# A two-layer hybrid diffusion step: one ScalarE copy per layer-norm tile in place of two activations, and private weight buffers for one up-projection unit

## The reference

```python
def post_norm(x, y, g, b):
    return layer_norm(ALPHA * x + y, g, b)

def modulate(x, shift, scale):
    return x * (1 + scale) + shift

def conv_ffn(h, w_up, conv_w, conv_b, w_down):
    u = dwconv3(h @ w_up, conv_w, conv_b)
    g, val = jnp.split(u, 2, axis=-1)
    return (jax.nn.silu(g) * val) @ w_down

# in each layer i, for context (p) and latent (s) tokens
xs = post_norm(xs, mod_s[2] * ys, ln_g[i, 0], ln_b[i, 0])
hs = modulate(xs, mod_s[3], mod_s[4])
fs = conv_ffn(hs, ffn_w_up[i], ffn_conv_w[i], ffn_conv_b[i], ffn_w_down[i])
xs = post_norm(xs, mod_s[5] * fs, ln_g[i, 1], ln_b[i, 1])
```

## Time and profile before

| | us |
|---|---|
| median of 3 timed runs | 1999.53 (1999.06 to 1999.94) |
| the profiled execution, its own time | 1995.32 |
| the span of its trace | 1993.4 |
| TensorE matmul busy | 1831.9 (92% of the span) |
| TensorE weight load busy | 1682.0 (84%) |
| VectorE busy | 1148.0 (58%) |
| ScalarE busy | 804.4 (40%) |
| GpSimd busy | 645.8 (32%) |
| TensorE waiting for GpSimd's L467, layer 0 and layer 1 | 3.3 and 3.4, once each |

### The profile page before, as it was taken

How to read it: one execution, slowest core, us unless ns; L and a number is a source line. 1 busy time by engine, 2 the same in 40 slices (tenths; PEclk the granted TensorE clock), 3 DMA queues, 4 the chain that set the end, 5 groups by cost and what they waited for, 6 DMA issues and landing times.

```text
span 1993.4 us, 31127 instructions
## 1 busy us (share of the span) xinstructions
PE 1831.9 (92%) x11636; PEld 1682.0 (84%) x11636; DVE 1148.0 (58%) x1634; ACT 804.4 (40%) x1203; POOL 645.8 (32%) x278
## 2 busy tenths in 40 slices
PE   6999999996889999999997799999789999999995
PEld 2338888885779999999996789888779999999995
DVE  6994667665447772277724645354456773177723
ACT  5982554554253331133325445355343332133323
POOL 0002212122355443333344231223355433333341
PEclk9999999997889999999998899999989999999998
DMA  9992111110112222122221111121111222122221
GB/s 386 359 362 72 49 40 48 51 44 18 42 43 74 71 74 87 53 74 74 90 73 32 48 56 46 48 64 38 32 53 62 75 75 80 57 74 74 86 73 53
DMA packets 49054, 164.94 MB, mean 83 GB/s; under 512 B 5584, under 2 KB 11216, under 8 KB 48848
## 3 DMA queue, kind: packets, MB, share of 16 engines
q1 hardware_dynamic: 42640, 159.68, 24.0%
q10 hardware_dynamic: 6336, 4.20, 0.7%
HBM read 159.12 MB, written 4.74 MB: 82 GB/s over the span
## 4 chain that ended last, share of the span: by engine, by line
PE 79%; DVE 9%; ACT 5%; issue 2%; DVEq 2%; DMA 2%; POOL 1%; ACTq 0%; SPq 0%; POOLq 0%
PE pj L511 66%; DVE alo L1537 2%; PE mO L881 2%; DMA awr<-in_w_ada 2%; PE psS L634 2%; PE psO L676 2%; PE psT L650 1%; DVE X L1620 1%; ACT h32t L1028 1%; PE prow L550 1%; PE psT L659 1%; DVE pr L1718 1%; DVEq L1619 1%; PE mS L837 1%; PE mT L844 1%
## 5 line engine op out<-in xcount | busy, mean ns | idle before, releaser
L408 POOL TENSOR_TENSOR wlo<-wraw,whi 128x1024 fp32r<-128x1024 f32 (+1 forms) x132 | 356.4, 2700 | 968.4 <-ACT whi L1013 968.4
L511 PE MATMUL pj<-Hh,whi 128*128 128x322 f32 x2432 | 584.8, 322 | 58.3 <-issue 19.4
L511 PE MATMUL pj<-Hl,whi 128*128 128x322 f32 x2432 | 566.8, 315 | 0.0
L511 PE MATMUL pj<-Hh,wlo 128*128 128x322 f32 x2432 | 562.9, 313 | 0.0
L511 PEld LDWEIGHTS pj<-Hh,whi 128*128 128x128 f32 x2432 | 412.6, 192 | 78.9 <-issue 54.2
L511 PEld LDWEIGHTS pj<-Hh,wlo 128*128 128x128 f32 x2432 | 417.2, 192 | 0.0
L511 PEld LDWEIGHTS pj<-Hl,whi 128*128 128x128 f32 x2432 | 417.1, 192 | 0.0
L1013 ACT CAST whi<-wraw 128x1024 fp32r<-128x1024 f32 (+1 forms) x184 | 203.9, 1108 | 302.3 <-PE pj L511 298.7
L1588 DVE SCALAR_TENSOR_TENSOR X<-pj,mods,X 128x129 f32<-128x129 f32 (+1 forms) x144 | 54.6, 435 | 284.6 <-PE pj L511 284.5
L1643 DVE SCALAR_TENSOR_TENSOR fcv<-fus,vec,fcv 128x644 f32<-128x644 f32 x88 | 172.5, 1960 | 15.1 <-issue 15.1
L1641 DVE SCALAR_TENSOR_TENSOR fcv<-fus,vec,fcv 128x644 f32<-128x644 f32 x88 | 166.4, 1891 | 15.2 <-issue 15.2
(11 more groups left out here) (298 smaller groups left out, 2354.1 us busy)
## 6 DMA issues: line engine op xcount, KB each, us to landing
awr<-in_w_ada SPq DMA_DIRECT2D x96, 512.0 KB, 5.6
wraw<-in_w_up SPq DMA_DIRECT2D x88, 512.0 KB, 3.6
wraw<-in_w_dn SPq DMA_DIRECT2D x32, 704.0 KB, 4.1
wraw<-in_w_qkv SPq DMA_DIRECT2D x24, 512.0 KB, 3.6
wraw<-in_w_mlin SPq DMA_DIRECT2D x24, 512.0 KB, 3.6
wraw<-in_w_wo SPq DMA_DIRECT2D x8, 512.0 KB, 3.5
wraw<-in_w_mlout SPq DMA_DIRECT2D x8, 512.0 KB, 3.6
X<-in_xT SPq DMA_DIRECT2D x1, 2576.0 KB, 16.7
```

What stands on the lines that cost most here:

```text
L408: nc.gpsimd.tensor_tensor(wlo[k][:, 0:width], wraw[k][:, 0:width], whi[k][:, 0:width].bitcast(F32), ALU.subtract).then_inc(w_lo, 1)
L511: last = mm(out[:, c, 0:HALF], w, x[:, j, c * HALF:(c + 1) * HALF], start=(j == 0 and n == 0), stop=(j == n_k - 1 and n == 2))
```

## The change

1. In `h_build`, the two activations that wrote `Hh[:, j]` from X are replaced by a drain (ScalarE waits until its pipeline is empty, because the copy reads what the activations just wrote) and one copy of `h32[j % 2]`, pads included, to `Hh[:, j]`.
2. Two new buffers `wnh` and `wnl` (128 x 1024 each) hold the high and low part of unit 2 of half 0 of each FFN. ScalarE copies `wraw[0]` to `wnh` before it reads out unit 0, without waiting for TensorE, and no longer splits unit 2 between the two read-outs. GpSimd's first step of `split_ffn` writes `wnl` and needs only `w_hi`. TensorE takes unit 2's weights from `wnh` and `wnl`. All later units use the double buffers as before.
3. For this, TensorE's second `up` pair is written out ahead of the loop in both halves, and the loop runs from 2.

```diff
--- before.py
+++ after.py
@@ -191,6 +191,8 @@
             fsg = sb("fsg", [P, TP], F32, s)
             fpr = sb("fpr", [P, TP], F32, s)
             sqj = [sb(f"sqj{k}", [P, TP], F32, s) for k in range(2)]
+            wnh = sb("wnh", [P, D], F32R, s)
+            wnl = sb("wnl", [P, D], F32R, s)
         with ExitStack() as s:
             awr = [sb(f"awr{k}", [P, 2, 512], F32, s) for k in range(AS)]
             ahi = [sb(f"ahi{k}", [P, 2, 512], F32R, s) for k in range(AS // 2)]
@@ -413,7 +415,11 @@
 
                 b = base + 2 * GH + KT
                 for j in range(KT):
-                    split_one(base + first + j, D)
+                    if j == 0:
+                        pool.wait_ge(w_hi, base + first + 1)
+                        nc.gpsimd.tensor_tensor(wnl[:, :], wraw[0][:, 0:D], wnh[:, :].bitcast(F32), ALU.subtract).then_inc(w_lo, 1)
+                    else:
+                        split_one(base + first + j, D)
                     residual(j)
                 split_run(base + first + KT, 2 * GH - first - KT, D)
                 split_run(base + 2 * GH, KT, WMAX)
@@ -492,7 +498,7 @@
         def _(pe):
             mm = nc.tensor.matmul
 
-            def tile(pair, k, ks, n_k=KT, src=None, pairs=1, read=None):
+            def tile(pair, k, ks, n_k=KT, src=None, pairs=1, read=None, spare=None):
 
 
                 v = 2 * pair + k
@@ -505,7 +511,7 @@
                     if read:
                         pe.wait_ge(*read)
                 for j in ks:
-                    wh, wl = whi[k][:, j * P:(j + 1) * P], wlo[k][:, j * P:(j + 1) * P]
+                    wh, wl = (w[:, j * P:(j + 1) * P] for w in spare or (whi[k], wlo[k]))
                     for n, (w, x) in enumerate(((wh, hi), (wh, lo), (wl, hi))):
                         for c in range(2):
                             last = mm(out[:, c, 0:HALF], w, x[:, j, c * HALF:(c + 1) * HALF],
@@ -581,16 +587,18 @@
                 for half in range(2):
                     b = base + half * (2 * GH + KT)
 
-                    def up(i):
+                    def up(i, spare=None):
                         for k in range(2):
-                            tile(b // 2 + i, k, FULL, pairs=2, read=(pj_copied, copied + 2 * i + k - 1))
+                            tile(b // 2 + i, k, FULL, pairs=2, read=(pj_copied, copied + 2 * i + k - 1), spare=None if k else spare)
                     copied, added = 3 * DA_HEADS + (2 * layer + half) * 2 * GH + layer * 6 * ML_HEADS, KT * (1 + 2 * layer + half + layer)
                     pe.wait_ge(pj_added, added + 2)
                     if half == 0:
                         first_pair(b // 2, KT, h_ready, KT * h_inst)
+                        up(1, (wnh, wnl))
                     else:
                         up(0)
-                    with pe.Fori(1, GH) as i:
+                        up(1)
+                    with pe.Fori(2, GH) as i:
                         up(i)
 
                     def down(i):
@@ -1026,9 +1034,8 @@
                         act.wait_ge(h_ready, KT * (n + 1) + j - 1)
                     for t0, t1, m in SPANS:
                         fn(h32[j % 2][:, t0:t1], X[:, j, t0:t1], ACT.Identity, scale=la[:, j, m:m + 1], bias=lb[:, j, m:m + 1])
-                    for t0, t1, m in SPANS:
-                        last = fn(Hh[:, j, t0:t1], X[:, j, t0:t1], ACT.Identity, scale=la[:, j, m:m + 1], bias=lb[:, j, m:m + 1])
-                    last.then_inc(h_hi, 1)
+                    act.drain()
+                    nc.scalar.copy(Hh[:, j, :], h32[j % 2][:, :]).then_inc(h_hi, 1)
 
             def square(n, j):
 
@@ -1073,10 +1080,14 @@
                     cnt = (2 * layer + half) * GH
 
                     def body(i, width=D):
+                        if half == 0 and isinstance(i, int) and i == 0:
+                            act.wait_ge(w_landed[0], 16 * (b // 2 + 2))
+                            nc.scalar.copy(wnh[:, :], wraw[0][:, 0:D]).then_inc(w_hi, 1)
                         if not isinstance(i, int) or cnt + i > 0:
                             act.wait_ge(conv_ready, 2 * cnt + 2 * i)
                         evac(b // 2 + i, 0, fus[0][:, 1:TP + 1], pairs=2)
-                        split(b // 2 + i + 1, 0, width)
+                        if half or not isinstance(i, int) or i > 0:
+                            split(b // 2 + i + 1, 0, width)
                         evac(b // 2 + i, 1, fus[1][:, 1:TP + 1], pairs=2)
                         split(b // 2 + i + 1, 1, width)
                         act.wait_ge(conv_ready, 2 * cnt + 2 * i + 1)
```

## The result

Over five runs of each kernel the median went from 1999.06 us to 1983.04 (1982.83 to 1983.50): ratio 0.9917 [0.9907, 0.9928], so 0.8% faster, which is clear of the noise. The forecast was 1988.2 with a range of 1984.5 to 1993.0, so the direction was right and the gain of 16.0 us was larger than the 11.35 of the sum, outside the range by 1.5. The profiled execution took 1983.50, its span is 1981.7.

A forecast was written before the change was run, and what follows sets the result against it. TensorE, busy 92% of the span, was taken as the bound. Gains of 3.91 (norm 0), 1.44 (norm 1), 4.53 (norm 2) and 1.47 (clock) sum to 11.35 us; 1999.53 - 11.35 = 1988.2, range 1984.5 to 1993.0.

The forecast's parts named there:

- Part 1, the copy: Three layer norms: ScalarE takes 1.96 us per tile instead of 2.18; gains 0.52, 1.44 and 1.13, sum 3.09 us.
- Part 2, the private buffers: TensorE's waits for unit 2 behind norms 0 and 2 go, giving 3.39 and 3.40 us.
- Unit 4: Its low part in each FFN would be ready 0.1 us early, costed at nothing; bounds 0 and 2.0 us each.
- The rival that made it a wait: VectorE's hold only moves, so TensorE waits 2.0 us for unit 4 in each FFN: 1992.1 us, chance 0.13.
- ScalarE as the pace: TensorE's slow start is shorter, so the norms give up to 1.8 us each: 1985.9 us, chance 0.06.
- instruction supply: Fetching TensorE's longer written-out code at four places stalls it by three packets each: 2003.5 us, chance 0.04.
- the change does little: Unit 2's weights come late after all, by 3 us twice; 3 to 4 us gained, 1996 us, chance 0.04.
- The clock behind norm 2's gap: Without the idle gap before unit 2, TensorE's clock does not fall behind norm 2: 1.47 us more.
- the rival that it would not be given back: The 1.47 us of clock behind norm 2 is not gained, or slow norm starts lengthen: 1989.7 us, chance 0.12.
- two gaps of equal size had different outcomes: TensorE's waits of 3.34 and 3.41 us before unit 2: the clock fell only behind the second, after norm 2.
- norm 0's gap: TensorE's wait of 3.34 us between norm 0 and unit 2, with unit 2's split and low part in between.
- the three stretches: The timelines around the three layer norms built by `h_build`, where the forecast placed all its gains, 11.35 us.

The follow-up runs named there:

- e1: Kernel before with the copy alone in the three norms, unit 2 still in the double buffer; 1993.96 us, ratio 0.9976 to before.
- e9: Kernel before with the copy in norm 1 only; 1995.40 us, ratio 0.9980 to before.
- e3: Kernel before without any edit, profiled and timed again; 1998.60 us, ratio 0.9997 to before.
- e5: Kernel before with nine small matmuls of constants after the first pair of units of each FFN, filling TensorE's gaps; 1998.28 us, ratio 0.9999 to before.
- e11: Kernel after with two idle ScalarE copies of constants ahead of the read-out of the gates behind norm 1; 1988.66 us, ratio 0.9945 to before.
- e10: Kernel after with the two old activations kept in norm 1 alone; 1988.36 us, ratio 0.9953 to before.
- e4: Kernel after without any edit, profiled and timed again; 1982.23 us, ratio 0.9915 to before.

## Why the prediction was right and wrong

- **Part 1, the copy.** Right in mechanism and size: 1.90 us per tile against 1.96, gain in norm 1 1.32 against 1.44 (0.96 and 1.08 where the copy stands without the buffers, e1 and e9). TensorE was the pace until the end, as said, and the early start was 0.30 against 0.23 (587.32 - 583.60 = 3.72 instead of 4.02).
- **Part 2, the private buffers.** Right: with part 1 3.78 and 4.77 against 3.91 and 4.53. The read-out of unit 0 is what is late next.
- **Unit 4.** Right: one hold of VectorE fewer, margin 0.8 instead of 0.1, no wait. The rival that made it a wait (1992.1) is wrong.
- **ScalarE as the pace** (1985.9), **instruction supply** (2003.5) and **the change does little** (1996) did not come: no gap of TensorE at a written-out pair, 54 packets against 51. The first is nearest to the number measured and yet not its cause, since the norms gave what was forecast for them.
- **The clock behind norm 2's gap.** Right, 1.56 against 1.47, and the rival that it would not be given back is wrong. The rule of the Trainium skill (TensorE: Matmul & The Clock Gate, Part 1: The HAM clock gate) that the monitor runs freely, which the forecast set behind that rival, agrees with these traces in that equal gaps had different outcomes; but within the program the clock's rises stood nearly in place. I let it speak in one direction only.
- **The first step that failed** is the forecast's reading of "two gaps of equal size had different outcomes" as one term of 1.47. Of the four traces that have norm 0's gap unfilled (before, e3, e1, e9) three show a fall behind it, of 2.4 to 2.7 us. The sum had nothing at norm 0; the traces want 2.4 there where the clock falls, beside 1.5 at norm 2. How often it falls in the timed executions is not shown, and e5, which removes both falls, moved its median by 0.5 only.
- **The second** is that the sum took every stage outside the three stretches as unchanged. The mLSTM's waits of 2.8 us do not change, but the clock's answer to them does once norm 1 ends 1.3 earlier: 3.0 to 4.6 us in the traces that no term or rival held. This is the step that the experiments bear out best: the copy in norm 1 alone brought 3.5 instead of 1.1 (e9), and a delay of 1.26 behind it cost 5.6 to 6.4 (e11).
- **Under both** lies a choice: the sum was made on one profiled execution, and the 4.21 us by which the median lies above it was added as a constant. It was not one. It is in part norm 0's fall of 2.4, which the trace happened to lack and the change takes away. A part stays: the short start, 1.6 to 4.5 less than in all traces but e10's, which the change does not touch. That the forecast for a profiled execution, 1983.97, lies so near to the 1983.50 measured is luck: the mLSTM gave 4.55 that it did not have, and the start took 4.40. 9.8 for the waits, 3.8 for the clock behind both gaps and 3.0 for the mLSTM (e3 against e4) are 16.7; a range that held these would have reached to 1982.8.

## What to carry to other kernels

The time of a wait and the time that the clock loses behind it are two terms, and here the second belonged to every wait of 2.8 to 3.4 us, fallen or not in the trace at hand: price each at its fall times a chance, and ask of each later wait that the change moves whether it falls or is spared. Where a median lies 4 us above the profiled execution, look for what that execution lacked before adding the difference as a constant. When a part's gain doesn't match its stretches, cut the traces of several kernels at the same instructions; the column that no edit touches is the one to explain.

## What was not expected of the hardware

- 1.26 us of delay at one place cost 5.6 to 6.4 us in the median (e11), and 3.1 us of matmuls in each of two gaps, which kept the clock there, gained only 0.5 (e5); the mLSTM, up to 740 us behind the first gap, had three falls where e3 has one.
- The last slow stretch ahead of norm 0 ends 58.5 to 58.7 us before the norm's head in twelve traces and 59.06 before it in before and e10: the granted clock follows the program this closely from one execution to the next.
- Behind equal waits of 2.83 and 2.84 us the same six matmuls took 1.51 and 0.84 us; the clock was at its lower level in the one case and not in the other.
- A drain and a copy that reads what was just written began 1.26 us after the pair of activations with fixed addresses, 1.33 where the addresses came from a register.
- The two stretches without such waits, 458 and 470.6 us long, agree within 0.1 us over all fourteen traces; what differs between executions lies in the other columns, where TensorE waits.
